# Adding the expert bias with a small product, and new slots and banks for the second layer

## The reference

```
logits = xt @ w_router + b_router
top_vals, top_idx = lax.top_k(logits, TOP_K)          # 4 of 32 experts
gates = softmax(top_vals)
...
h = xblk @ w1[e] + b1[e]                              # 1024 -> 2048
x_glu = minimum(h[..., ::2], 7.0)
x_lin = clip(h[..., 1::2], -7.0, 7.0)
act = x_glu * sigmoid(1.702 * x_glu) * (x_lin + 1.0)
y = act @ w2[e] + b2[e]                               # 1024 -> 1024
...
out[token] += y * gate
```

## Time and profile before

| | |
|---|---|
| median of 3 runs | 2398.59 us (2397.43 to 2401.11) |
| the profiled execution | 2405.35 us, its span 2403.6 us |
| granted TensorE clock, mean | 0.956 |
| TensorE busy | 2197.8 us, 91% |
| DVE busy | 1519.1 us, 63% |
| ACT busy | 973.7 us, 41% |
| POOL busy | 285.7 us, 12% |
| DMA, hardware queue | 467.84 MB, 54.4% of 16 engines |
| loads of weight slots | 390, 1 MB each, 7.2 us from issue to landing |
| loads of `b1b` | 33, 1 MB written each, 10.9 us to landing |

### The profile page before, as it was taken

One profiled execution on the slowest core, in us unless ns is written; L12 is line 12 of the kernel. 1 busy time (PEld: TensorE's weight loads), 2 busy tenths in 40 slices (PEclk: granted clock), 3 DMA queues, 4 the chain that ended last, 5 costly groups with the idle time before them and its releaser, 6 DMA issues. The chain is left out here.

```text
span 2403.6 us, 29704 instructions
## 1 busy us (share of the span) xinstructions
PE 2197.8 (91%) x9492; PEld 1596.8 (66%) x9493; DVE 1519.1 (63%) x1969; ACT 973.7 (41%) x1146; POOL 285.7 (12%) x245
## 2 busy tenths in 40 slices
PE   6999587997689998999899999999899999999997
PEld 4454277544357876686586868686566886886885
DVE  4013566333677677777777777677777677677776
ACT  3023444011254444444444444444444444444443
POOL 1000300001101110111011111111012011011111
PEclk9999789898799999999999999999999999999998
DMA  7000200200598669868978786867998668668666
GB/s 242 0 1 11 85 1 1 88 27 29 203 354 290 232 223 355 328 240 304 350 273 294 261 304 229 290 236 292 332 336 317 223 238 302 239 209 303 236 215 230
DMA packets 244996, 524.28 MB, mean 218 GB/s; under 512 B 17575, under 2 KB 22759, under 8 KB 240736
## 3 DMA queue, kind: packets, MB, share of 16 engines
q1 hardware_dynamic: 220990, 467.84, 54.4%
q0 software_dynamic: 23904, 55.95, 6.3%
q10 hardware_dynamic: 66, 0.02, 0.0%
HBM read 522.20 MB, written 32.11 MB: 231 GB/s over the span
## 5 line engine op out<-in xcount | busy, mean ns | idle before, releaser
L1469 DVE TENSOR_TENSOR w_lo<-ring,w_hi 128x2048 fp32r<-128x2048 f32 x330 | 754.7, 2288 | 256.3 <-ACT w_hi L711 255.9
L711 ACT ACTIVATE w_hi<-ring 128x2048 fp32r<-128x2048 f32 x327 | 624.9, 1916 | 441.4 <-PE ps L1031 421.4
L1029 PE MATMUL ps<-w_hi,xT_hi 128*128 128x512 f32 x1212 | 499.2, 412 | 11.3 <-DVE xT_lo L1469 9.9
L1031 PE MATMUL ps<-w_hi,xT_lo 128*128 128x512 f32 x1212 | 474.6, 392 | 0.0
L1030 PE MATMUL ps<-w_lo,xT_hi 128*128 128x512 f32 x1212 | 473.1, 390 | 0.0
L1029 PE MATMUL ps<-w_hi,actT_hi 128*128 128x512 f32 x720 | 303.6, 422 | 80.4 <-issue 79.7
L1030 PE MATMUL ps<-w_lo,actT_hi 128*128 128x512 f32 x720 | 294.1, 409 | 0.0
L1031 PE MATMUL ps<-w_hi,actT_lo 128*128 128x512 f32 x720 | 294.0, 408 | 0.0
L1029 PEld LDWEIGHTS ps<-w_hi,xT_hi 128*128 128x128 f32 x1212 | 228.2, 188 | 76.2 <-issue 18.0
L1030 PEld LDWEIGHTS ps<-w_lo,xT_hi 128*128 128x128 f32 x1212 | 228.5, 189 | 53.1 <-issue 9.1
L1031 PEld LDWEIGHTS ps<-w_hi,xT_lo 128*128 128x128 f32 x1212 | 227.8, 188 | 49.9
(11 more groups left out here) (260 smaller groups left out, 2121.3 us busy)
## 6 DMA issues: line engine op xcount, KB each, us to landing
ring<-in_w SPq DMA_DIRECT2D x390, 1024.0 KB, 7.2
b1b<-in_b SPq DMA_DIRECT2D x33, 1024.0 KB, 10.9
xh<-in_x SPq DMA_DIRECT2D x2, 2048.0 KB, 18.0
work<-in_w_out SPq DMA_DIRECT2D x1, 4096.0 KB, 12.7
token_rows<-uT POOLq DMA_DIRECT2D x8, 512.0 KB, 2.9
out<-xh SPq DMA_DIRECT2D x8, 512.0 KB, 2.6
work<-in_w_in SPq DMA_DIRECT2D x2, 1536.0 KB, 19.5
uT<-in_w_mem_kv SPq DMA_DIRECT2D x1, 2048.0 KB, 18.1
```

The source lines that it names most:

```text
L711: act_e.activation(w_hi[s % SPLIT][:, :, :], slot(s), ACT.Copy).then_inc(hi_ready, counted(s, whole))
L1029: pe.matmul(acc, hi, whi, start=first, stop=False)
L1031: return pe.matmul(acc, lo, whi, start=False, stop=last)
L1469: return dve.tensor_tensor(lo, x, hi.bitcast(F32), ALU.subtract)
```

## The change

It does four things.

1. The bias is no longer loaded in each pass. All 32 rows of `b1` are loaded once, twice over, into 64 partitions; ACT and DVE make of them `b1w`, whose partitions 0 to 31 hold the high parts and 32 to 63 the low parts. In each pass DVE makes `sel`, 64 by 128, with ones in rows e and e + 32 (the sum of two columns of the identity, broadcast). One product `sel` by `b1w` of 512 columns then adds the bias in PSUM, in front of the second slot of each quarter and in each group. DVE clamps straight from PSUM; `hb` and `b1b` are gone, and `h_free` is signalled behind the second clamp.
2. Slot 3 is split in singles too: `WHOLE` is `(5, 7)` where it was `(3, 5, 7)`.
3. A second-layer slot holds two k-tiles of all 1024 columns. `down(s)` makes both column halves, needs only quarter s - 8 of the activations, and `combine(0)` may start when the first half of slot 11 is done (`y_half`).
4. In singles the output has banks 1 and 4, the next tokens are transposed into banks 5 and 6, and the token ids go to bank 3. The waits of `down` for `h_free` and for `xlo_ready` stand in doubles only; there the latter comes ahead of the second column half of slot 8.

The rest of the diff passes the bank numbers on to `take_xhi`, `take_xlo`, `transpose_x`, `token_ids` and `make_idx`.

```diff
@@ -51,7 +51,7 @@
 RAW = 6
 SPLIT = 4
 LEAD = 3
-WHOLE = (3, 5, 7)
+WHOLE = (5, 7)
 AHEAD_OOB = 1 << 20
 
 
...
@@ -176,6 +176,7 @@
         gates, posm = (a[:, :, :].rearrange("p a b -> p (a b)")[:, 0:NT * E].rearrange("p (t e) -> p t e", t=NT)
                        for a in (km, vm))
         gatesT, b2_sb = uT[:, 11, :], uT[:, 12, :]
+        b1_raw = uT[0:2 * E, 0:2, :].rearrange("p a b -> p (a b)")
 
 
 
+        b1w = sb("b1w", [2 * E, 2 * FF], F32R)
         actT_hi, actT_lo = ([sb(f"{n}{g}", [P, KD, P], F32R) for g in range(2)] for n in ("actT_hi", "actT_lo"))
-        hb = sb("hb", [P, 2, HALF])
+        sel = sb("sel", [2 * E, P], F32R)
         glu, lin, gel, act = (sb(n, [P, 2, 2, HALF // 2]) for n in ("glu", "lin", "gel", "act"))
-        b1b = sb("b1b", [P, 2 * FF])
...
@@ -278,6 +280,16 @@
         def whole_of(groups):
 
             return WHOLE if len(groups) == 1 else ()
+
+        def next_x_bank(groups):
+
+            return 5 if len(groups) == 1 else 4
+
+        def ids_bank(groups):
+            return 3 if len(groups) == 1 else 6
+
+        def y_bank(groups, g, b):
+            return 4 * b + g if len(groups) == 2 else 1 + 3 * b
 
         def counted(s, whole):
 
@@ -337,9 +349,9 @@
                 if s < 8:
                     src = w1v[bass.ds(e, 1), :, 4 * (s % 2):4 * (s % 2) + 4, HALF * (s // 2):HALF * (s // 2) + HALF]
                 else:
-                    kh, b = (s - 8) // 2, s % 2
-                    src = w2v[bass.ds(e, 1), :, 4 * kh:4 * kh + 4, HALF * b:HALF * b + HALF]
-                sp.dma_start(slot(s), src.rearrange("o p k c -> (o p) k c")).then_inc(slot_in[s % RAW], 16)
+                    src = w2v[bass.ds(e, 1), :, 2 * (s - 8):2 * (s - 8) + 2, :]
+                dst = slot(s) if s < 8 else slot(s).rearrange("p (k b) c -> p k (b c)", k=2)
+                sp.dma_start(dst, src.rearrange("o p k c -> (o p) k c")).then_inc(slot_in[s % RAW], 16)
 
 
             sp.wait_ge(ylru, 2 * LT)
@@ -353,6 +365,8 @@
             sp.wait_ge(op_done, 6 * NT)
             sp.wait_ge(padded, 2)
             sp.dma_start(b2_sb[0:E, :], b2[0]).then_inc(b2_in, 16)
+            for half in range(2):
+                sp.dma_start(b1_raw[half * E:(half + 1) * E, :], b1[0]).then_inc(b1_in, 16)
             sp.wait_ge(ttab_ready, 1)
             for s in range(4, RAW):
                 load_slot(0, s)
@@ -360,27 +374,15 @@
                 sp.wait_ge(init_ready, 2 * i + 2)
                 sp.dma_start(out[0, i * P:(i + 1) * P, :], xh[:, i, :]).then_inc(init_out, 16)
             sp.wait_ge(init_out, 16 * NT)
-            sp.dma_start(b1b[:, :], b1[0, 0:1, :].to_broadcast([P, 2 * FF])).then_inc(b1_in, 16)
             total = sp.value_load(ttab[0:1, TALL:TALL + 1], min_val=1, max_val=NPASS)
-            hfa_reg, hfb_reg = (sp.alloc_register(n) for n in ("hfa", "hfb"))
             with sp.Fori(0, total) as p:
                 e_now = sp.value_load(ttab[0:1, bass.ds(p + TE, 1)], min_val=0, max_val=E - 1)
                 e_next = sp.value_load(ttab[0:1, bass.ds(p + (TE + 1), 1)], min_val=0, max_val=E - 1)
-                doubles = sp.value_load(ttab[0:1, bass.ds(p + (TDBL + 1), 1)], min_val=0, max_val=NPASS)
 
                 for s in range(RAW, RAW + NSLOT):
 
                     sp.wait_ge(raw_done[s % RAW], p * (NSLOT // RAW) + s // RAW)
                     load_slot(e_now if s < NSLOT else e_next, s % NSLOT)
-
-                sp.reg_mul(hfa_reg, p, 4)
-                sp.reg_add(hfa_reg, hfa_reg, 6)
-                sp.reg_mul(hfb_reg, doubles, 4)
-                sp.reg_add(hfb_reg, hfb_reg, 2)
-                hfa, hfb = sp.snap(hfa_reg), sp.snap(hfb_reg)
-                sp.wait_ge(h_free[0], hfa)
-                sp.wait_ge(h_free[1], hfb)
-                sp.dma_start(b1b[:, :], b1[0, bass.ds(e_next, 1), :].to_broadcast([P, 2 * FF])).then_inc(b1_in, 16)
 
         @block.gpsimd
         def _(po):
...
@@ -690,7 +692,10 @@
                 act_e.wait_ge(slot_in[s], 16)
                 act_e.activation(w_hi[s][:, :, :], slot(s), ACT.Copy).then_inc(hi_ready, 1)
             act_e.wait_ge(ttab_ready, 1)
-            take_xhi(1, 0)
+            take_xhi(1, 0, 4)
+            act_e.wait_ge(b1_in, 32)
+            act_e.wait_ge(lg_done, NT)
+            act_e.activation(b1w[:, :], b1_raw, ACT.Copy).then_inc(b1_hi, 1)
             act_e.wait_ge(init_out, 16 * NT)
             total = act_e.value_load(ttab[0:1, TALL:TALL + 1], min_val=1, max_val=NPASS)
             with act_e.Fori(0, total) as p:
...
@@ -1075,6 +1080,11 @@
                             if j == 0:
                                 pe.wait_ge(xlo_ready[g], nth[g] + 1)
                         acc = ps[:, 2 * (j % 2) + g, :]
+                        if kh == 1:
+                            if j == 0:
+                                pe.wait_ge(b1_lo, 1)
+                                pe.wait_ge(sel_ready, p + 1)
+                            pe.matmul(acc, sel[:, :], b1w[:, j * HALF:(j + 1) * HALF], start=False, stop=False)
                         for k in range(4):
                             kk = 4 * kh + k
                             if s in whole:
@@ -1089,31 +1099,34 @@
                                 m.then_inc(w_used, counted(s, whole))
 
                     def down(s):
-                        kh, b = (s - 8) // 2, s % 2
+                        j = s - 8
                         wait_words(s)
-                        for g in groups:
-                            if kh == 0 and b == 0:
-                                pe.wait_ge(h_free[g], pieces[g] + 5)
-                            if kh == 0 and b == 1:
+                        for b in range(2):
+                            if j == 0 and b == 1 and len(groups) == 2:
                                 pe.wait_ge(xlo_ready[0], p + 2)
-                            for k in range(4):
-                                kk = 4 * kh + k
-                                if k % 2 == 0:
-                                    pe.wait_ge(alo_ready[g], pieces[g] + (kk // 2 + 1))
-                                m = three(ps[:, 4 * b + g, :], actT_hi[g][:, kk, :], actT_lo[g][:, kk, :],
-                                          w_hi[s % SPLIT][:, k, :], w_lo[s % SPLIT][:, k, :], kk == 0, kk == KD - 1)
+                            for g in groups:
+                                if j == 0 and b == 0 and len(groups) == 2:
+                                    pe.wait_ge(h_free[g], pieces[g] + 5)
+                                if b == 0:
+                                    pe.wait_ge(alo_ready[g], pieces[g] + (j + 1))
+                                for k in range(2):
+                                    m = three(ps[:, y_bank(groups, g, b), :], actT_hi[g][:, 2 * j + k, :],
+                                              actT_lo[g][:, 2 * j + k, :], w_hi[s % SPLIT][:, 2 * k + b, :],
+                                              w_lo[s % SPLIT][:, 2 * k + b, :], j == 0 and k == 0, j == 3 and k == 1)
+                            if j == 3 and b == 0:
+                                m.then_inc(y_half, 1)
                         m.then_inc(w_used, counted(s, whole))
 
                     up(0, 0)
                     pe.wait_ge(idx_ready, p + 1)
                     if len(groups) == 2:
-                        transpose_x(1)
+                        transpose_x(1, 6)
                         up(1, 0)
                         up(0, 1)
-                        token_ids(p + 2)
+                        token_ids(p + 2, ids_bank(groups))
                         up(1, 1)
                     else:
-                        token_ids(p + 2)
+                        token_ids(p + 2, ids_bank(groups))
                         up(1, 0)
                     for s in range(2, 8):
                         for g in groups:
...
@@ -1492,7 +1505,10 @@
             for s in range(LEAD):
                 dve.wait_ge(hi_ready, s + 1)
                 minus_hi(w_lo[s][:, :, :], slot(s), w_hi[s][:, :, :]).then_inc(raw_done[s], 1)
-            take_xlo(1, 0)
+            take_xlo(1, 0, 4)
+            dve.wait_ge(b1_hi, 1)
+            minus_hi(b1w[E:2 * E, :], b1_raw[E:2 * E, :], b1w[E:2 * E, :]).then_inc(b1_lo, 1)
+            dve.wait_ge(b1_lo, 1)
             dve.wait_ge(init_out, 16 * NT)
             with dve.Fori(0, total) as p:
                 e = dve.value_load(ttab[0:1, bass.ds(p + TE, 1)], min_val=0, max_val=E - 1)
@@ -1506,6 +1522,8 @@
 
                 dve.wait_ge(combined[0], p * 2 + 2)
                 dve.wait_ge(combined[1], dbl * 2 + 2)
+                dve.tensor_tensor(sel[:, :], ident[0:2 * E, bass.ds(e, 1)].to_broadcast([2 * E, P]),
+                                  ident[0:2 * E, bass.ds(e + E, 1)].to_broadcast([2 * E, P]), ALU.add).then_inc(sel_ready, 1)
                 dve.wait_ge(xg_in, p * 32 + 32)
                 dve.tensor_copy(gate_cur[:, :].rearrange("p (g a) -> p g a", a=1),
                                 xg[:, :, bass.ds(e + D, 1)]).then_inc(gate_copied, 1)
...
```

(18 more changed lines are left out.)

56 lines of the change are left out of this document (27 added, 29 removed).

## The result

The change made the kernel slower: 2452.23 us (2448.91 to 2453.46) against 2399.31 for the kernel before on the same chip, a ratio of 1.0217 [1.0204, 1.0229]. The prediction said 2355, 97 us less. The profiled execution took 2448.91 us, its span 2447.2, its mean granted clock is 0.965.

The account below looks back on a forecast made before the run. It took singles to be bound by a ring of waits through DVE, scatter and TensorE, doubles by TensorE alone. 2405.35 - 100 (singles) + 50 (doubles) + 5 (clock) + 1 (prologue) = 2361, median 2355 us; 8-in-10 range 2327 to 2402.

Parts of the forecast that it names:

- I take 0.228: TensorE: each 64-row bias product costs one ordinary product's start, 0.228 us; four add 0.91 a single, eight 1.8 a double.
- The split of slot 3: Start of singles: the added split, 2.2 us on DVE and 1.9 on ACT, hides in DVE's 4.44 us idx_cur wait.
- the ring behind a single: combine(1), scatter, idx_cur, make_idx, DVE's queue, TensorE's second layer bound a single; shortened to 37.6 to 38.9, taken as 39.0.
- the wait for `xT_lo`: Singles, before slot 9: TensorE's 5.1 us stall goes, leaving at most half to one us at the last transposes.
- the new stall in doubles: Middle of slot 8: its second half writes bank 4 and waits 2.0 us for xT_lo in each double.
- the clock: Doubles: the granted clock may fall after the new stall, bounds 0 and 20 us; a quarter taken, +5.
- Rival (a): The new stall lowers the clock in every double: 15 us more, 2370; chance 0.16.
- the clamps: DVE: a clamp from PSUM takes about 0.42 us, the next starts 0.33 on; worth nothing in a double.
- the prologue: Before the loop: b1's loads, ACT's copy and DVE's difference come ahead of the first bias product, +1 us.
- (c): Rival: singles' stall moves to transpose_act(3), slot 3's split not being hidden; singles gain 1, total 2436; chance 0.10.

Follow-up runs that it names:

- the run that cured it: Changed kernel, but in singles VectorE waits until GpSimd has issued the last scatter before starting slot 3's split: 2416.67 us, 1.0077.
- the best version: Changed kernel with 128-row bias products, doubles' second output half in banks 2 and 3, and slot 3's split waiting for the scatter's issue: 2345.07 us, 0.977.
- the needless work: Kernel before the change plus two unused 1024-column VectorE ops at the head of each single: 2405.8 us, 1.0025.

## Why the prediction was wrong, step by step

It was made on spans as -100 + 50 + 5 + 1 = -44 us. The spans differ by 2447.2 - 2403.6 = +43.6, so 88 us are to be explained; the rest of the 97 is that the profiled execution stood 6.8 above its median before and 3.3 under it after. By the passes: the doubles took 94 us more and not 55, which is 39; the singles gained 46 and not 100, which is 54; the loop began 4 us sooner and not 1 later, which takes off 5.

- **The step that failed first: "I take 0.228, that of the nearest row, since its 512 columns are the same."** The term was to be +1.8 a double and is +4.6 (76.7 with 64 rows against 73.9 with 128); 13 x 2.8 = 36 us. The bounds (nothing and 0.228) were both too low, because the nearest row was of a product whose neighbours have its shape. The row that would have warned lay beside it: a weight load runs under the product ahead. What changes between two products can break that, and this was not costed. In singles where nothing else holds TensorE it is 0.8 a pass: 39.6 with 64 rows, 38.8 with 128, both with the wait for the scatter's issue.
- **The step that failed second: "The split of slot 3 ... in the same place; cost nothing".** Its own time was hidden, though the 4.44 us that were to hide it belong to singles behind a single, but I did not ask what else runs in that place. The kernel starts its scatter there. Singles behind a double were forecast at 38.4 and took 43.1; 3.4 us of it goes with the order of two instructions (9 x 3.4 = 31 us; the medians of the run that cured it differ by 36), 0.8 is the first step, and 0.4 the forecast's 38.4 against the 38.8 of the best version.
- **Right in kind, short in size: the ring behind a single.** VectorE's walk from `make_idx` to the end of `combine(1)` was forecast at 29.4; after, it goes from 1132.83 to 1162.25, which is 29.4. The rest, scatter and `idx_cur`, was put at 8.2 to 9.5 and is 10.7 (1162.25 to 1172.93), so the pass is 40.1 and not 39.0: 10 us in nine passes. The 8.2 was that of the quickest of nine: from the scatter's start to `idx_cur` it took 7.1 us there and 8.1 to 9.3 in the eight others, before the change. VectorE in that pass and at the head of the next:

```profile
1132.83 0.16 DVE L1476 TENSOR_SCALAR pad<-ps 128x2 f32<-128x2 f32 x1 [4.32 <-POOL idx_cur L502]
...
1161.51 0.74 DVE L1581 SCALAR_TENSOR_TENSOR rows<-ps,gate_cur,rows 128x512 f32<-128x512 f32 x1
...
1172.93 0.16 DVE L1476 TENSOR_SCALAR pad<-ps 128x2 f32<-128x2 f32 x1 [4.60 <-POOL idx_cur L502]
```

  Taken together the singles gained 46 us (19 x 44.0 less 19 x 41.6), not 100.
- **Right: the wait for `xT_lo`.** The 4 to 5 us stall of every single is gone, some 1 us stands at the last transposes behind a single, as forecast, and 1.8 to 2.3 behind a double.
- **Right: the new stall in doubles,** 2.0 forecast and 2.0 measured. With 128 rows the double is 73.9, as summed.
- **Right in kind: the clock.** A quarter of the doubles was assumed, 5 of 13 fell: 5 x 1.7 = 8.5 us, not 5. Rival (a), all of them, is refuted by the other 8.
- **Right: the clamps.** The same view as before gives 418 ns for one from PSUM, and the next starts 0.33 on, as in `DVE L1551` at 1284.84 and `L1552` at 1285.17. The saving on VectorE is real and worth nothing in a double, as said.
- **Not decided: the prologue.** +1 was forecast; the loop begins 4.3 us sooner after than before (638.4 against 642.7). But over the twelve profiled executions it begins between 635.1 and 644.1, and in the kernel before with the needless work at 636.9, so one pair says nothing of 1 us.
- **The rivals.** None had the cause. (c) named slot 3's split as the thing not hidden and came nearest in time (2436), but by another mechanism: the split's own 2.2 us on VectorE, for a gain of 1 us a single. Behind single passes the split did cost nothing.

## What to carry over

Ask of "free" idle time not only whether the moved work fits in, but who starts something beside it: an op that was put into a wait made the very thing waited for later. Read the wait in the same kind of pass that the work goes into. A mean far from its median (1417 and 1020 ns for the scatters) means two populations: find what parts them. Price a new instruction by a row with the same neighbours, not just the same size, above all on an engine that prepares the next instruction under the current one. And where a lightly used engine issues a transfer in the chain that bounds the pass, the order of that issue and a neighbour's long op can be worth more than the op itself.
